# Hybrid attention and SSD block on one core: one C-times-B product per group, values of two heads in one product, state product ahead of the transposes, fourth tile's state products and last normalisation later

## The chip, the cores and the metric

The kernel runs on one core of one Trainium2 chip. The core has five engines with a queue each: TensorE (PE, matrix products), VectorE (DVE), ScalarE (ACT), GpSimd (POOL) and SyncE (SP, which issues the transfers). Each works through its own instructions in order; they wait for each other by semaphores. Time is device time of one execution in microseconds (us), lower is better. Products write into PSUM, eight banks of 128 partitions by 512 floats (2 KB); all else lies in SBUF.

## The reference

One layer over 512 positions of width 1024, in float32:

```python
u = rmsnorm(h, mix_pre_norm)
q, k, v, z, xbc, dt_raw, g_a, g_b = split(u @ w_in)
y_attn = banded_sink_attention(rope(q), rope(k), v, sinks) @ w_attn_out   # 16 heads, 4 groups, window 128
# SSD branch, 32 heads of 64 in 4 groups, state 128:
xs, B, C = split(silu(causal_dwconv(xbc)))
dt = softplus(dt_raw + bias); a_cs = cumsum(dt * a)          # within a chunk
y_diag = ((C @ B.T) * exp(a_cs[l] - a_cs[s]), lower triangle) @ (x * dt)
states = B.T @ (x * dt * decay);  prev = scan(prev * chunk_decay + states)
y_off  = (C @ prev) * exp(a_cs)
y = group_rmsnorm((y_diag + y_off + x * d_skip) * silu(z)) * ssd_norm
y_ssd = y @ w_ssd_out
h = h + rmsnorm((sigmoid(g_a) * y_attn + sigmoid(g_b) * y_ssd) @ w_out)
h = h + rmsnorm((silu(conv(gate)) * conv(value)) @ w_down)   # channel mixer, d_ff 2816
```

## The kernel before

**Tiling.** The 512 positions are four tiles (`NT` = 4) of 128. Each big product is made of three passes: weights are split on chip into a rounded high half `whi` (ScalarE, L482, function `hi`) and a rest `wlo` (VectorE, L863, function `lo`), and so are the activations. Weight blocks of 128x2048 come through two buffers `raw0`, `raw1`; block n can be split when it has landed and when TensorE has finished with block n-2 in that buffer. The semaphore `lo_done` counts finished low halves.

**Group loop.** Attention and SSD run in four groups (`NG` = 4; 4 query heads and 8 SSD heads each), Python loops that write each engine's instructions out in order. A group projects q, k, v (two weight blocks, a product group per tile), then B, C, x with their convolution, then turns B and x to rows of positions (`tok`). Then comes the tile loop, t = 0 to 3, in which TensorE does for each tile:

- `C times B` (L1552) into bank 6, masked by VectorE (`masked_cb`, L1090) into `cb_m`;
- the attention scores (L1565, four products) into banks 4 and 5;
- a quarter of the gate projection z (`z_tile`, 24 products of 512 columns), for t = 0 also the rest of `tok`;
- `turn_p`: the transposes of the probabilities (L1410) into bank 4, copied to `pT` by ScalarE (L692);
- for t > 0 the state products (L1393 with `c_dec` and `state`): the carried state times C scaled by growth;
- the decay products (L1393 with `decay_m` and `xdt`, `diagonal`), which end the tile's y (semaphore `y_mm`);
- for t < 3 the state product (L1589): B times `xdtd`, into bank 7, for the carried state;
- `weigh_values` (L1422): values times `pT`, eight products of 64 columns, into bank 4, copied to `oT` by ScalarE (L696).

The decay and values products have 64 columns of weights and write to partitions 0 to 63 and 64 to 127 in turn.

**The other engines.** After `y_mm` ScalarE makes the next tile's gains from the summed decays (L569, L575). VectorE takes the maximum of the scores (L1071 to L1074), multiplies the gains by `cb_m` (L1062), makes `xdt` = x times dt (L1086), divides the probabilities (L1078 to L1080), forms the gate (L1054), adds up y (L1113) and updates the state: times its decay (L1120), plus bank 7 (L1121). GpSimd makes `xdtd` (L439) and `c_dec`, C times growth for the next tile (L444), for which it waits until the tile's `y_mm`. The fourth tile's scores and state products come last in the group's loop; its decay products, transposes and values are laid between the next group's first projection tiles.

**After the groups.** `gate_a(i)`, i = 0 to 3: gate products (banks 0, 1) and attention-output products (banks 2, 3), 24 each, i = 0 outside and the others in a loop on every engine. The attention outputs `oT` are split into `rhi`, `rlo` first, then the SSD outputs `yT` (`split_y`, L1134), tiles 0 to 7 of them before the loop and 8 to 15 behind it. The last group's normalisation (`sum_squares`, `norm_sums`, roots by GpSimd, a trip of the roots through DRAM to spread them, `normalize` L977) stands in VectorE's queue behind `gate_a(0)`, ahead of the low halves of i = 1. Then come the SSD output products, the merge, w_out and the channel mixer, which are unchanged.

## Time and profile before

| | |
|---|---|
| median of 3 runs | 1061.54 us (1061.15 to 1063.48) |
| profiled execution, its own time | 1061.45 us |
| its span (first to last instruction) | 1059.7 us |
| mean granted TensorE clock | 0.996 |
| TensorE products busy | 1033.1 us (97%), 5423 records |
| VectorE busy | 640.1 us (60%) |
| ScalarE busy | 472.4 us (45%) |
| GpSimd busy | 86.9 us (8%) |
| mean of the low halves (L863) | 2.24 us |

The span is what the trace covers; the time has 1.75 us more around it. A product in plain float32 leaves two records in the trace, a product of the rounded halves one. Ends of products are modelled, so neighbouring rows overlap and a stretch is best measured from start to start.

### The profile page before, as it was taken

What the parts mean: (1) busy time and instruction counts of PE and PEld (TensorE: products, weight loads), DVE (VectorE), ACT (ScalarE), POOL (GpSimd) and SP (SyncE); (2) the same over time, 40 slices, a digit from 0 to 9 for tenths busy, and PEclk for the clock granted to TensorE, in tenths of its full rate; (3) what the DMA queues carried; (4) which work ended last, traced back from release to release, by engine and by line L of the source; (5) the groups of instructions that cost most, each with busy time, mean ns of one, the idle gap of its engine ahead of it and who ended that gap; (6) DMA issues with size and microseconds to landing.
All of it is one profiled execution on the core that took longest, in us unless ns stands there. A gap on an engine that the chain in (4) does not pass through costs nothing.

```text
span 1059.7 us, 14004 instructions
## 1 busy us (share of the span) xinstructions
PE 1033.1 (97%) x5423; PEld 863.8 (82%) x5423; DVE 640.1 (60%) x851; ACT 472.4 (45%) x835; POOL 86.9 (8%) x132
## 2 busy tenths in 40 slices
PE   8999999999999999989999999999999999999997
PEld 7887888798779877768888888798888888888886
DVE  4878787878787878642523223676766666651214
ACT  5657647655764576512312132554344343422112
POOL 6002101200120021000000003110000000000001
PEclk9999999999999999989999999999999999999999
DMA  6333351343334323232232344421243333332211
GB/s 193 120 126 109 111 148 50 118 133 109 97 103 143 106 100 120 50 111 87 87 112 79 119 158 152 127 71 50 79 114 83 97 101 82 116 119 80 98 62 79
DMA packets 117978, 111.26 MB, mean 105 GB/s; under 512 B 13279, under 2 KB 108075, under 8 KB 117931
## 3 DMA queue, kind: packets, MB, share of 16 engines
q1 hardware_dynamic: 117931, 110.61, 33.8%
q8 instruction: 32, 0.52, 0.2%
q14 instruction: 15, 0.12, 0.0%
HBM read 108.36 MB, written 2.24 MB: 104 GB/s over the span
## 4 chain that ended last, share of the span: by engine, by line
PE 88%; DVE 5%; ACT 3%; DMA 2%; issue 1%; POOL 1%; SPq 0%; DVEq 0%; POOLq 0%; ACTq 0%
PE ps L1292 20%; PE ps L1294 20%; PE ps L1293 20%; PE ps L1299 7%; PE ps L1301 6%; PE ps L1300 6%; PE ps L1393 2%; PE ps L1565 1%; DVE wlo L863 1%; DVE sm L1078 1%; PE ps L1589 1%; DVE state L1120 1%; PE ps L1422 1%; PE ps L1410 1%; ACT x_tok L557 1%
## 5 line engine op out<-in xcount | busy, mean ns | idle before, releaser
L863 DVE TENSOR_TENSOR wlo<-raw,whi 128x2048 fp32r<-128x2048 f32 (+2 forms) x83 | 185.9, 2242 | 198.3 <-ACT whi L482 198.3
L1292 PE MATMUL ps<-uhi,whi 128*128 128x512 f32 x768 | 301.4, 393 | 0.0
L1294 PE MATMUL ps<-uhi,wlo 128*128 128x512 f32 x768 | 299.2, 390 | 0.0
L1293 PE MATMUL ps<-ulo,whi 128*128 128x512 f32 x768 | 298.9, 389 | 0.0
L482 ACT ACTIVATE whi<-raw 128x2048 fp32r<-128x2048 f32 (+2 forms) x83 | 155.8, 1878 | 187.6 <-PE ps L1301 99.0
L1294 PEld LDWEIGHTS ps<-uhi,wlo 128*128 128x128 f32 x768 | 144.2, 188 | 30.4
L1293 PEld LDWEIGHTS ps<-ulo,whi 128*128 128x128 f32 x768 | 144.3, 188 | 29.1
L1292 PEld LDWEIGHTS ps<-uhi,whi 128*128 128x128 f32 x768 | 144.3, 188 | 29.2 <-issue 0.2
L1240 DVE SCALAR_TENSOR_TENSOR yT<-ps,fpar,yT 128x511 f32<-128x511 f32 x88 | 65.8, 749 | 37.5 <-ACT yT L820 35.9
L1292 PE MATMUL ps<-rhi,whi 128*128 128x512 f32 x192 | 75.8, 395 | 6.2 <-DVE wlo L863 6.2
L820 ACT ACTIVATE yT<-ps,fpar 128x512 f32<-128x512 f32 x44 | 34.2, 780 | 98.9 <-DVE fpar L1235 68.0
L1293 PE MATMUL ps<-rlo,whi 128*128 128x512 f32 x192 | 75.6, 394 | 0.0
L1294 PE MATMUL ps<-rhi,wlo 128*128 128x512 f32 x192 | 75.4, 393 | 0.0
L1299 PE MATMUL ps<-whi,rhi 128*128 128x512 f32 x176 | 68.5, 389 | 0.0
L1300 PE MATMUL ps<-whi,rlo 128*128 128x512 f32 x176 | 68.5, 389 | 0.0
L1301 PE MATMUL ps<-wlo,rhi 128*128 128x512 f32 x176 | 68.5, 389 | 0.0
L991 DVE SCALAR_TENSOR_TENSOR conv<-ps,par,conv 128x511 f32<-128x511 f32 (+2 forms) x72 | 53.9, 748 | 18.2 <-ACT conv L545 16.5
L1299 PE MATMUL ps<-whi,uhi 128*128 128x384 f32 (+2 forms) x176 | 64.2, 365 | 0.6 <-DVE wlo L863 0.6
L1301 PE MATMUL ps<-wlo,uhi 128*128 128x384 f32 (+2 forms) x176 | 62.7, 357 | 0.0
L1300 PE MATMUL ps<-whi,ulo 128*128 128x384 f32 (+2 forms) x176 | 62.6, 356 | 0.0
L545 ACT ACTIVATE conv<-ps,par 128x512 f32<-128x512 f32 x24 | 18.7, 778 | 68.7 <-PE ps L1294 68.7
L1292 PEld LDWEIGHTS ps<-rhi,whi 128*128 128x128 f32 x192 | 36.6, 190 | 14.2 <-DVE wlo L863 6.6
(226 smaller groups left out, 1370.5 us busy)
## 6 DMA issues: line engine op xcount, KB each, us to landing
raw<-in_w_in_dram SPq DMA_DIRECT2D x24, 1024.0 KB
raw<-in_w_up_dram SPq DMA_DIRECT2D x44, 512.0 KB
raw<-in_w_down_dram SPq DMA_DIRECT2D x11, 1024.0 KB
raw<-in_w_in_dram SPq DMA_DIRECT2D x16, 512.0 KB
sums_bc<-sum_rows_scratch SPq DMA_DIRECT2D x16, 512.0 KB, 4.2
raw<-in_w_ssd_out_dram SPq DMA_DIRECT2D x8, 1024.0 KB
grow_bc<-sum_rows_scratch SPq DMA_DIRECT2D x12, 512.0 KB, 5.7
raw<-in_w_attn_out_dram SPq DMA_DIRECT2D x4, 1024.0 KB
```

Source lines behind the costliest of these rows:

```text
L482: act.activation(whi[sl][:, 0:width] if into is None else into, raw[sl][:, 0:width], ACT.Copy).then_inc(s["hi_done"], 1)
L820: act.activation(work[:, v, :], bank(2 * q + v), ACT.Identity, scale=fpar[:, q, FTAPS - 1, v:v + 1], bias=fpar[:, q, FTAPS, v:v + 1]).then ...
L863: dve.tensor_tensor(wlo[sl][:, 0:width] if into is None else into, raw[sl][:, 0:width], h.bitcast(F32), ALU.subtract).then_inc(s["lo_done" ...
L991: ins = dve.scalar_tensor_tensor(out=conv[:, f, sh:], in0=ps[:, 4 + f % 4, 0:S - sh], scalar=cw[:, k, at:at + 1], in1=conv[:, f, sh:], op0 ...
L1240: ins = dve.scalar_tensor_tensor(out=work[:, v, sh:], in0=ps[:, 2 * q + v, 0:S - sh], scalar=fpar[:, q, k, v:v + 1], in1=work[:, v, sh:], ...
L1292: pe.matmul(bank(b)[:, span], hi_[:, k, c], ah[:, span], start=first and k == 0, stop=False)
L1293: pe.matmul(bank(b)[:, span], hi_[:, k, c], al[:, span], start=False, stop=False)
L1294: ins = pe.matmul(bank(b)[:, span], lo_[:, k, c], ah[:, span], start=False, stop=last and k == KD - 1)
L1299: pe.matmul(o, ah, wh, start=first, stop=False)
L1300: pe.matmul(o, al, wh, start=False, stop=False)
L1301: return pe.matmul(o, ah, wl, start=False, stop=last)
L1393: ins = pe.matmul(ps[r, 2 + t % 2, (h // 2) * P:(h // 2 + 1) * P], weights[:, h * HD:(h + 1) * HD], moving[:, h, :], start=first if t == 0 ...
```

## The change

Seven edits, all in the attention and SSD stage and in `gate_a`.

1. C times B for all four tiles is done in one batch of four products into bank 6, after `tok(1)`, and VectorE masks the four at once into `cb_m`, which now lies in the q columns of `qkv_sb`.
2. `weigh_values` does two heads in one product: four products of 2x64 columns instead of eight of 64. They go to bank 6, so the next scores wait for `pT_sb` only, no longer for `o_sb`.
3. The state product (L1589) moves from behind the decay products to right behind `z_tile`, ahead of `turn_p`.
4. The fourth tile's state products (`from_state`) move from behind its scores to right in front of its decay products, behind the next group's first projection tile. A new semaphore `off_mm` marks their end.
5. VectorE scales the state (`scaled`) as soon as `off_mm` is there, before the sum into yT. GpSimd's `c_dec` waits for `scaled` where it waited for `y_mm`, and at a group's first tile also for the low half of the block that VectorE splits there.
6. VectorE's order in a tile is maximum, masked gains, x times dt, division, gate in all tiles; at t = 0 the gate came before the division. ScalarE does the first gate's tanh ahead of its copies.
7. In the last group and `gate_a`: the products `features(1, ...)` stand between `turn_p` and `weigh_values`; five of the attention outputs are split earlier (`O_ORDER`); VectorE's order is gate_a(0), split_y 0 to 7, gate_a(1), normalize, gate_a(2), split_y 8 to 13, gate_a(3), split_y 14 and 15. `Y_TILE` gives the split SSD outputs 8 to 13 tiles of their own, so that they need not wait for the attention products to end. The loops of VectorE and ScalarE over i are written out.

TensorE's queue between the first and second tile of the second group, before (`whi`, `wlo` gate products end; names as above):

```order
L1294 MATMUL ps<-uhi,wlo 128x512
L1410 MATMUL ps<-ident,probs 128x128 x4
L1393 MATMUL ps<-decay_m,xdt 64x128 x8
L1589 MATMUL ps<-xdtd,b_tok 128x512
L1422 MATMUL ps<-pT,qkv_sb 64x64
L1422 MATMUL ps<-pT,va 64x64
...
L1552 MATMUL ps<-conv 128x128
L1565 MATMUL ps<-kB,qB 128x128 x4
```

and in the changed kernel:

```order
L1321 MATMUL ps<-uhi,wlo 128x512
L1616 MATMUL ps<-xdtd,b_tok 128x512
L1437 MATMUL ps<-ident,probs 128x128 x4
L1420 MATMUL ps<-decay_m,xdt 64x128 x8
L1453 MATMUL ps<-pT,qkv_sb 64x2x64 x2
L1453 MATMUL ps<-pT,va 64x2x64 x2
L1603 MATMUL ps<-kB,qB 128x128 x4
```

The state product has moved ahead of the transposes, the values are four instructions instead of eight, and C times B (L1552) is gone from between values and scores.

VectorE's queue in `gate_a`, with what each row waits for. Before, from the first block's gates to the first low half of the second block:

```order
L1153 SCALAR_TENSOR_TENSOR oT<-gt,ps 128x512 [waits at_mm,ga_tanh]
L1153 SCALAR_TENSOR_TENSOR oT<-gt,ps 128x512 [waits blk_done,ga_tanh]
L977 TENSOR_TENSOR yT<-yT,conv 128x512 [waits roots_in]
L977 TENSOR_TENSOR yT<-yT,conv 128x512 x3
L1134 SCALAR_TENSOR_TENSOR rlo<-yT,par,rhi 128x512 [waits split_hi] x4
...
L863 TENSOR_TENSOR wlo<-raw,whi 128x2048 [waits hi_done]
```

and now:

```order
L1170 SCALAR_TENSOR_TENSOR oT<-gt,ps 128x512 [waits at_mm,ga_tanh]
L1170 SCALAR_TENSOR_TENSOR oT<-gt,ps 128x512 [waits blk_done,ga_tanh]
L1156 SCALAR_TENSOR_TENSOR rlo<-yT,par,rhi 128x512 [waits split_hi] x8
L887 TENSOR_TENSOR wlo<-raw,whi 128x2048 [waits hi_done] x2
L1170 SCALAR_TENSOR_TENSOR oT<-gt,ps 128x512 [waits at_mm,ga_tanh]
L1170 SCALAR_TENSOR_TENSOR oT<-gt,ps 128x512 [waits blk_done,ga_tanh]
L1001 TENSOR_TENSOR yT<-yT,conv 128x512 [waits roots_in]
L1001 TENSOR_TENSOR yT<-yT,conv 128x512 x3
```

The normalisation (`roots_in`) has moved behind the low halves and gates of the second block.

The diff, cut to its core:

```diff
@@ semaphores, names
-        cb_m = sb("cb_m", [P, P], where=gctx)
+        cb_m = qkv_sb[:, :, 0:P]
+        O_ORDER = (1, 2, 3, 4, 5, 0, 6, 7)
+        Y_TILE = tuple(range(KD)) + tuple(range(2 * KD, KF)) + tuple(range(KD, 2 * KD + KI - KF))
@@ gpsimd
-                    pool.wait_ge(s["y_mm"], T + 1 if t else T)
+                    if t:
+                        pool.wait_ge(s["scaled"], G * (NT - 2) + t)
+                    else:
+                        pool.wait_ge(s["y_mm"], T)
+                        pool.wait_ge(s["lo_done"], G * PER_G + 7)
                     pool.tensor_tensor(c_dec[:, :, :], grow_bc[:, :, :], ...
@@ scalar
+            hi_gate(0)
+            square_y(NG - 1)
+            gates_a(0)
+            act.wait_ge(s["yn_ok"], KD)
+            for k in range(KD):
+                split_y(k)
             mean_y(NG - 1)
+            for i in range(1, NG):
+                hi_attention(i)
+                gates_a(i)
+                hi_gate(i)
+                if i == 2:
+                    act.wait_ge(s["yn_ok"], KI)
+                    for k in range(KD, KF - KD):
+                        split_y(k)
@@ vector, after silu(5)
+                dve.wait_ge(s["cb_mm"], G + 1)
+                dve.tensor_tensor(cb_m, bank(6).rearrange("p (t l) -> p t l", t=NT), tri..., ALU.mult).then_inc(s["cbm_ok"], 1)
@@ vector, tile loop
+                    if 0 < t < NT - 1:
+                        dve.wait_ge(s["off_mm"], G * (NT - 1) + t)
+                        dve.tensor_tensor(h8(state[:, :]), h8(state[:, :]), heads(dec[:, 2, t, group_heads(G)], SH, HD),
+                                          ALU.mult).then_inc(s["scaled"], 1)
+                        dve.wait_ge(s["scaled"], G * (NT - 2) + t)
+                        dve.wait_ge(s["st_mm"], G * (NT - 1) + (t + 1))
+                        dve.tensor_tensor(state[:, :], state[:, :], bank(7), ALU.add).then_inc(s["st_ok"], 1)
                     dve.wait_ge(s["y_mm"], T + 1)
@@ tensor
+                for half in (1, 0):
+                    cols = slice(64 * half, 64 * half + 64)
+                    v = qkv_sb[:, t, QW + KW:QW + 2 * KW] if half else va[:, t, :]
+                    for a in range(2):
+                        o = ps[64 * a:64 * a + 64, 6, 0:2 * P].rearrange("p (f c) -> p f c", f=2)[:, :, cols]
+                        ins = pe.matmul(o, v, pT[:, 2 * a:2 * a + 2, cols], start=True, stop=True)
+            def from_state(G, t):
+                T = G * NT + t
+                pe.wait_ge(s["st_ok"], G * (NT - 1) + t)
+                pe.wait_ge(s["grown"], G * (NT - 1) + t)
+                if T > 1:
+                    pe.wait_ge(s["y_done"], T - 1)
+                if t == 1:
+                    pe.wait_ge(s["tok_sb"], G * 5 + 3)
+                products(G, t, state, c_dec, True, False).then_inc(s["off_mm"], 1)
@@ tensor, next group's first tile
                         if h == 0 and t == 0:
+                            from_state(G - 1, NT - 1)
                             diagonal(G - 1, NT - 1)
@@ tensor, after tok(1)
+                for t in range(NT):
+                    c = slice(t * P, (t + 1) * P)
+                    ins = pe.matmul(ps[:, 6, c], conv[:, 0, c], conv[:, 1, c], start=True, stop=True)
+                ins.then_inc(s["cb_mm"], 1)
@@ tensor, tile loop
-                        pe.wait_ge(s["o_sb"], T)
+                        pe.wait_ge(s["pT_sb"], T)
...
                         pe.matmul(bank(7), b_tok[:, c], xdtd[:, :], start=True, stop=True).then_inc(s["st_mm"], 1)
+                        turn_p(G, t)
+                        if t:
+                            from_state(G, t)
+                        diagonal(G, t)
                         weigh_values(G, t)
```

## Rows read from the trace of the kernel before

**Rows 1.** Waits of TensorE: waiter, released by: us in total, times, longest

```profile
PE ps L1292 <- DVE wlo L863: 6.2, 1, 6.2
PE ps L1393 <- DVE state L1121: 3.1, 4, 1.2
PE ps L1410 <- DVE probs L1080: 2.6, 4, 0.7
...
PE ps L1422 <- ACT pT L692: 0.7, 1, 0.7
```

**Rows 2.** Timeline, TensorE, second group, first tile: start, us, instruction, [idle before]

```profile
183.69 0.39 PE L1293 MATMUL ps<-ulo,whi 128*128 128x512 f32 x1
183.91 0.39 PE L1294 MATMUL ps<-uhi,wlo 128*128 128x512 f32 x1
184.96 0.66 PE L1410 MATMUL ps<-ident,probs 128*128 128x128 f32 x4 [0.66 <-DVE probs L1080]
185.54 1.09 PE L1393 MATMUL ps<-decay_m,xdt 128*64 128x128 f32 x16
186.57 1.12 PE L1589 MATMUL ps<-xdtd,b_tok 128*128 128x512 f32 x2
187.62 0.34 PE L1422 MATMUL ps<-pT,qkv_sb 128*64 128x64 f32 x4
...
188.29 0.49 PE L1552 MATMUL ps<-conv 128*128 128x128 f32 x2
188.88 1.13 PE L1565 MATMUL ps<-kB,qB 128*128 128x128 f32 x8
189.76 0.48 PE L1292 MATMUL ps<-uhi,whi 128*128 128x512 f32 x1
```

**Rows 3.** Timeline, VectorE, second group

```profile
181.55 2.41 DVE L1078 TENSOR_TENSOR sm<-sm 128x4 f32<-128x4 f32 x1 [0.60 <-ACT sm L663]
...
205.16 1.44 DVE L1080 TENSOR_TENSOR probs<-probs,sm 128x512 f32<-128x512 f32 x1
...
210.30 2.14 DVE L1120 TENSOR_TENSOR state<-state,dec 128x512 f32<-128x512 f32 x1
...
214.48 1.29 DVE L1062 TENSOR_TENSOR decay_m<-decay_m,cb_m 128x512 f32<-128x512 f32 x2
215.69 0.68 DVE L1086 TENSOR_TENSOR xdt<-x_tok,dt_s 128x512 f32<-128x512 f32 x1
```

**Rows 4.** Timeline, GpSimd, second group

```profile
181.53 2.41 POOL L444 TENSOR_TENSOR c_dec<-grow_bc,conv 128x1024 f32<-128x1024 f32 x1
...
205.00 1.04 POOL L439 TENSOR_TENSOR xdtd<-xdt,dec 128x512 f32<-128x512 f32 x1 [4.65 <-DVE xdt L1086]
```

**Rows 5.** Timeline, TensorE, second group, fourth tile

```profile
211.45 1.13 PE L1565 MATMUL ps<-kB,qB 128*128 128x128 f32 x8
213.22 1.09 PE L1393 MATMUL ps<-c_dec,state 128*64 128x128 f32 x16 [0.64 <-DVE state L1121]
```

**Rows 6.** Timeline, ScalarE, gains of the fourth tile

```profile
209.34 1.28 ACT L569 ACTIVATE decay_m<-sums_bc,sum_s 128x128 f32<-128x128 f32 x4 [1.39 <-PE ps L1393]
210.97 0.38 ACT L696 ACTIVATE oT<-ps 128x256 f32<-128x256 f32 x1 [0.34 <-PE ps L1422]
...
212.41 1.14 ACT L575 ACTIVATE decay_m<-decay_m 128x512 f32<-128x512 f32 x2
```

**Rows 7.** Timeline, TensorE, the long wait of the last group

```profile
455.38 0.80 PE L1292 MATMUL ps<-rhi,whi 128*128 128x512 f32 x1 [6.18 <-DVE wlo L863]
455.97 0.63 PE L1293 MATMUL ps<-rlo,whi 128*128 128x512 f32 x1
```

**Rows 8.** Chain that ended last, 434 to 456: start, us, what

```profile
441.23 5.19 DMA conv<-roots_scratch
...
447.43 3.04 DVE yT L977 x3
```

**Rows 9.** Windows: busy us of each engine, granted clock (PEclk), DMA share, GB/s

```profile
core 0: us, PE busy (x) PEld busy (x) DVE busy (x) ACT busy (x) POOL busy (x), PEclk, DMA share, GB/s
...
455.00:461.00 6.00, 5.62 (x15) 4.44 (x16) 2.52 (x2) 0.00 (x0) 0.00 (x0) 0.57 0.76 249
```

More of the change, by code:

```diff
@@ L688, in group @@
                         hi_next(7, 4 * QKV if G < NG - 1 else BLK)
+                        if G == NG - 1:
+                            for k in O_ORDER[0:5]:
+                                split_o(k)
                     else:
@@ L705, in _, with split_y, gates_a @@
             act.wait_ge(s["o_sb"], NG * NT)
-            for k in range(KD):
-                act.activation(rhi[:, KD + k, :], oT[:, k, :], ACT.Copy).then_inc(s["split_hi"], 1)
+            for k in O_ORDER[5:]:
+                split_o(k)
             SN = 0
-            act.wait_ge(s["yn_ok"], KD)
-            for k in range(KD):
-                act.activation(rhi[:, k, :], yT[:, k, :], ACT.Copy, scale=par[:, 1, SN + k:SN + k + 1]).then_inc(s["split_hi"], 1)
-            square_y(NG - 1)
-            def gate_a(i, first=False):
+            def split_y(k):
+                act.activation(rhi[:, Y_TILE[k], :], yT[:, k, :], ACT.Copy, scale=par[:, 1, SN + k:SN + k + 1]).then_inc(s["split_hi"], 1)
+            def gates_a(i):
                 n = i * 2 + N_C1
-                if not first:
-                    hi(1, 64 * (i + (N_C1 // 2 + 1)), n)
                 for m in range(2):
@@ L1114, in group @@
                                       ALU.add).then_inc(s["y_done"], 1)
-                    if t < NT - 1:
-                        dve.wait_ge(s["st_mm"], G * (NT - 1) + (t + 1))
-                        if t == 0:
-                            dve.tensor_copy(state[:, :], bank(7)).then_inc(s["st_ok"], 1)
-                        else:
-                            link(dve.tensor_tensor(h8(state[:, :]), h8(state[:, :]), heads(dec[:, 2, t, group_heads(G)], SH, HD), ALU.mult))
-                            dve.tensor_tensor(state[:, :], state[:, :], bank(7), ALU.add).then_inc(s["st_ok"], 1)
+                    if t == 0:
+                        dve.wait_ge(s["st_mm"], G * (NT - 1) + 1)
+                        dve.tensor_copy(state[:, :], bank(7)).then_inc(s["st_ok"], 1)
                 if G < NG - 1:
@@ L1152, in gate_a @@
                         dve.wait_ge(s["blk_done"], n + 2)
-                    dve.scalar_tensor_tensor(out=oT[:, bass.ds(i * 2 + m, 1), :], in0=gt[:, m:m + 1, :], scalar=1.0,
+                    dve.scalar_tensor_tensor(out=oT[:, i * 2 + m:i * 2 + m + 1, :], in0=gt[:, m:m + 1, :], scalar=1.0,
                                              in1=ps[:, 2 + m:3 + m, :], op0=ALU.add, op1=ALU.mult).then_inc(s["at_ok"], 1)
-            gate_a(0, True)
-            normalize(NG - 1)
-            for k in range(KD // 2, KD):
-                split_y(k, KD + k + 1)
-            with dve.Fori(1, NG) as i:
-                gate_a(i)
-            for k in range(KD, KI):
-                split_y(k, KD + k + 1)
+            for at in range(5):
+                split_o(at)
+            gate_y(NG - 1)
+            for at in range(5, KD):
+                split_o(at)
+            lo(0, N_C1 + 3)
+            sum_squares(NG - 1)
+            gate_a(0)
+            for k in range(KD):
+                split_y(k)
+            gate_a(1)
+            normalize(NG - 1)
+            gate_a(2)
+            for k in range(KD, KF - KD):
+                split_y(k)
+            gate_a(3)
+            for k in range(KF - KD, KI):
+                split_y(k)
             before = links["n"]
@@ L1284, in tiles, with features @@
                 return w.rearrange("p (k n) -> p k n", k=k)
-            def features(b, sl, m, acts, first=True, last=True, span=slice(0, S), split=None):
+            def features(b, sl, m, acts, first=True, last=True, span=slice(0, S), split=None, ks=tuple(range(KD))):
                 hi_, lo_ = (tiles(w, KD) for w in split or (whi[sl][:, :], wlo[sl][:, :]))
-                for k in range(KD):
+                for k in ks:
                     ah, al = acts(k)
                     c = slice(m * P, (m + 1) * P)
-                    pe.matmul(bank(b)[:, span], hi_[:, k, c], ah[:, span], start=first and k == 0, stop=False)
+                    pe.matmul(bank(b)[:, span], hi_[:, k, c], ah[:, span], start=first and k == ks[0], stop=False)
                     pe.matmul(bank(b)[:, span], hi_[:, k, c], al[:, span], start=False, stop=False)
-                    ins = pe.matmul(bank(b)[:, span], lo_[:, k, c], ah[:, span], start=False, stop=last and k == KD - 1)
+                    ins = pe.matmul(bank(b)[:, span], lo_[:, k, c], ah[:, span], start=False, stop=last and k == ks[-1])
                 return ins
@@ L1522, in tok @@
                     else:
-                        pe.wait_ge(s["cbm_ok"], G * NT + 1)
+                        pe.wait_ge(s["cbm_ok"], G + 1)
                     for t in range(NT):
```

122 lines of the change are left out of this document (48 added, 74 removed).

## The prediction

> **What bounds the kernel now.** I read the page's engine table, then the view of waits for TensorE, then TensorE's rows in order of time around each wait, and last the other engines in the same stretches. The reader is to see that TensorE is busy nearly all of the 1059.7 us, so that time can only go where it has no product to run, where it runs a product badly packed, or where its clock is low. The profiled execution took 1061.45 us and the median of the runs is 1061.54 us, so sums made on the trace carry over as they are.
>
> The waits are few [rows 1]: one of 6.2 us for the low half of a weight block, four for the state (3.1 us in all), four for the probabilities (2.6 us) and one of 0.7 us for the turned probabilities. Everything between them is products back to back. Ends of products are modelled, so I measure by starts: neighbouring 512-column products start 0.23 us apart [rows 2].
>
> **Part 1: state product first, at a group's first tile.** The transposes of the probabilities start 1.05 us after the last gate product where 0.23 is ordinary: 0.82 us lost, in each of four groups [rows 2]. VectorE finishes the probabilities late because a 128x4 addition took 2.41 us [rows 3], exactly while GpSimd ran its 2.41 us scaling of C [rows 4]. The change puts the 512-column state product in this place. It needs only xdtd, which GpSimd had finished when it started on C, 3.4 us before the transposes began. And GpSimd's scaling of C now waits for the low half of a weight block, so the addition is free of it. I take all of 4 x 0.82 = 3.3 us. Late next would again be the probabilities: the addition may now wait for GpSimd's 1.04 us for xdtd instead of 2.41, its queue is shorter by the gate (0.7), and the transposes come 0.9 us later behind the state product, so some 2 us are left to them.
>
> The Trainium skill, in SBUF — State Buffer, section on port contention rules, says that GpSimd and a VectorE instruction with two SBUF inputs take the shared port pair as a lock for the whole instruction, and the later one blocks fully. The trace agrees (2.41 beside 2.41). By that rule the scaling of C is harmless in its new place too, since the gate, the sum into yT and the copy of the state each read PSUM for one input; a rule that blocked all of VectorE would cost up to 2.4 us of VectorE time a group there.
>
> **Part 2: the fourth tile's state products later.** After the scores of the fourth tile (211.45) the state products start at 213.22, 1.77 us later, where four score products cost 0.88 [rows 2, 5]: 0.88 lost. Rows 1 give 3.1 us for the four by modelled ends, 0.64 for this one; with 0.24 added to each that is 4.1 us. The cause is the state's scaling on VectorE, 2.14 us instead of some 0.7, again beside GpSimd [rows 3]. Afterwards the state is scaled before GpSimd may start, and the products stand behind one tile of projection (twelve products of 384 columns, 12 x 0.17 = 2.1 us and 0.2 of changes; in the last group a block of 24, 5.5 us). All 4.1 us go.
>
> But the products with the decay follow at once, and used to have this projection tile between them and the state products as well as before them. They need the gains. ScalarE's chain from the first gain (209.34) to the last exponential (213.55) is 4.21 us, with 0.34 of waiting for the values' copy that goes [rows 6], so about 3.85; then half of the masking (0.65 of 1.29) and x times dt (0.6 more) [rows 3]: 5.1 us. ScalarE starts 0.2 us after TensorE ends the third tile's decay products, so they can run 5.3 us after that end. TensorE gets there after values 0.56, scores 0.95, projection tile 2.3 and state products 0.93: 4.7 us. **New wait** 0.6 us in three groups (0 to 1.0 each): minus 1.8 us. In the last group the 5.5 us block covers it. Queued behind it on TensorE is everything; nothing else on its queue could run.
>
> Also, state and decay products now stand side by side, which saves two changes of array layout per group. One change costs about 0.1 us (below); with the slow first product after each, 0.25 a group, 1.0 us (0 to 1.4).
>
> **Part 3: C times B once per group.** Now one such product stands alone in each tile: 188.29 to 188.88, 0.59 us, the last 0.2 to 0.3 of it waiting for the values' copy out of bank 4, which the scores overwrite [rows 2]. The values go to bank 6 now, so this wait goes with it. Twelve of these leave (tiles two to four): 7.1 us. They return in the group's batch at the price of a score product, 0.88 / 4 = 0.22: 12 x 0.22 = 2.6. The scores then come directly behind 64-column products and pay the exposed weight load that C times B paid: I take 0.07 each, 0.8 in all (0 to 1.2). Net 7.1 - 2.6 - 0.8 = 3.7 us. VectorE masks all four at once, which lies under the 5.6 us of gate products.
>
> **Part 4: layout changes around the state product.** It stands between two groups of 64-column products and takes 1.05 us (186.57 to 187.62), where four products of 128 columns, the same columns, take 0.88 [rows 2]. The 0.17 is what two changes of layout cost it; the decay products before it pay about 0.1 more at their end. Moved behind the gate products and ahead of the transposes it has full-width neighbours. 12 x (0.17 + 0.1) = 3.3 us; from 0 (if 512 columns cost that anywhere) to 3.6.
>
> The Trainium skill, TensorEngine Tiling (Array Packing), section Key Properties, says a change of tiling mode drains the engine while a change of tile does not. By it the 3.3 us stand; without it only the part that is not a drain would, nearly 0. The row (0.17 us over) leans to the rule.
>
> **Part 5: values of two heads together.** Sixteen records of 64 columns take 0.67 us (187.62 to 188.29). Sixteen of 128 columns in the decay products take 1.03 (185.54 to 186.57), pairs side by side [rows 2]; eight of them take half of 0.93 and 0.1 for the layout: 0.56. 16 tiles x 0.11 = 1.8 us (0 to 2).
>
> **Part 6: the last group.** The 0.7 us wait for the turned probabilities [rows 1] gets a block of products laid between: 0.7 us.
>
> The large one: TensorE waits 6.18 us by the modelled end, 0.39 - 0.23 more by starts, 6.34 us, until 455.38 [rows 7]. VectorE's low half is queued behind the normalisation, which waits for a broadcast of the roots, 5.19 us from 441.23, and then spends 3.04 on three of its four products [rows 8] and four splittings more. After the wait TensorE starts products 0.43 apart, and its granted clock is 0.57 over the 6 us from 455 [rows 7, 9]: some are at 1.2 GHz, the engine having been idle just before. To 460.2 that is 12 products, 2.35 us more than at 0.23. Afterwards VectorE does the second block's low half before the normalisation, and the roots are then long there. I follow the queues for the next thing to be late: the low half for the attention products of the second block is due 11 us after its gate products start (436 to 447 on the old clock); ahead of it stand eight splittings of the size of x times dt [rows 3] (8 x 0.7 = 5.6 us) and its own 2.3 (a bound, that of the table's 2.24 us mean), so it is ready about 443 to 444. Slack 3 us. The normalisation's outputs are first used by ScalarE two blocks later. 6.34 + 2.35 = **8.7 us**.
>
> **Sum.** 3.3 + 4.1 - 1.8 + 1.0 + 3.7 + 3.3 + 1.8 + 0.7 + 8.7 = 24.8 us. 1061.45 - 24.8 = **1036.7 us**. With every unknown at its better end 1032; with all at the worse end 1045.
>
> **Rivals.**
> A. GpSimd loses the lock. For the state product GpSimd must multiply xdt by the decay (1.04 us) while VectorE divides the probabilities. Before, GpSimd came first: the multiplication by the inverse sum took 1.44 us beside it [rows 3, 4]. If VectorE is first, GpSimd ends up to 1 us later. From the end of the decay products, xdtd is due after 0.56 + 0.95 + 5.6 = 7.1 us and is ready at 5.3 + 0.1 + 1.04 = 6.4; one more and TensorE waits 0.3 to 0.4 at 12 tiles: 4 us, 1041. For it: the slack is only 0.7. Against: xdt ends before the last exponential that the division needs. By the rule of the Trainium skill cited in part 1 it would be a whole instruction that GpSimd waits for.
> B. The end wait is only moved: the low half for the second block slips by more than its 3 us of slack (ScalarE has eight splittings and four squares in front). A wait of 3 us and again the low clock, 2.35: 1042. Against: no transfer is ahead of it.
> C. Layout changes and values give nothing (3.3 + 1.8 + 1.0 lost): 1043. For it: none of these is a measured alternative; against, 0.17 and 0.11 are in the rows.
> D. Slower. The path from the decay products through gains, mask, xdt and GpSimd to the state product becomes the bound. It used to have state product, values and C times B beside it, 2.3 us; now only the values lie ahead of the scores. It has 0.7 us of slack; the change is a loss once each of twelve tiles waits over 24.8 / 12 = 2.1 us, so the path would have to be 2.8 us longer than the 6.4 its rows give, from GpSimd and VectorE blocking each other two or three times a tile. At 3 us a tile: 1073.
> E. The change does not do what it says, since a wait left in place holds the old order (the copy of the values to bank 6 against the transposes there, say): near 1058.
>
> **How the numbers follow.** Forecast 0.74, A 0.08, B 0.06, C 0.07, D 0.03, E 0.02. The range reaches A, B and C: 1031.5 to 1044. Time within 0.2% (2.1 us) cannot be told from no change. Faster by more than that: all but D and part of E, 0.95; same 0.02; slower 0.03.
>
> **What would show it.** Right: no idle ahead of the first tile's transposes, nor after the fourth tile's scores; 0.3 to 1 us ahead of the fourth tile's decay products in three groups; state product at 0.9 us, values at 0.56, C times B eight records in 0.9; clock at 1.00 from 437 to 467; no release by the normalisation. Wrong: TensorE waiting for GpSimd's xdtd at each tile (A or D), for a low half near 440 (B), or the state product still at 1.05 (C).

## The result and the profile after

| | before | changed |
|---|---|---|
| median | 1062.32 us, 4 runs (1061.15 to 1063.48) | 1036.14 us, 4 runs (1035.75 to 1037.94) |
| profiled execution, its own time | 1061.45 us | 1036.33 us |
| its span | 1059.7 us | 1034.5 us |
| mean granted TensorE clock | 0.996 | 0.998 |

The ratio of the times is 0.9757, with a 95% interval of 0.974 to 0.9774. 1036.7 us had been forecast, 24.8 us less than the profiled execution before; the profiled execution took 25.1 us less, and the medians differ by 26.2 us. The forecast stood on a median of 1061.54 us over three runs; with the fourth it is the 1062.32 us of the table.

The page first: the engine table and TensorE's clock in 40 slices.

```profile
PE 1019.5 (99%) x5295; PEld 860.9 (83%) x5295; DVE 622.3 (60%) x839; ACT 470.3 (45%) x835; POOL 86.4 (8%) x132
...
PEclk9999999999999999999999999999999999999999
```

TensorE's waits in the changed kernel (us in total, times, longest), without three of the kind of the last ones:

```profile
PE ps L1420 <- DVE xdt L1112: 2.4, 3, 0.8
PE ps L1343 <- POOL ones L373: 2.0, 1, 2.0
PE ps L1319 <- DVE ulo L907: 1.8, 2, 1.0
...
PE ps L1372 <- ACT uhi L499: 0.5, 1, 0.5
```

All four entries of [rows 1] are gone. One is new, the first: the products with the decay wait for x times dt, three times. The others stand in the start and at the change of stage, as before. The view lists idle time by modelled ends, and a wait of some 0.15 us does not show in it.

TensorE in the second group, from the first tile's gate products to the next ones (start, us, instruction). It answers to [rows 2]:

```profile
181.21 0.39 PE L1321 MATMUL ps<-uhi,wlo 128*128 128x512 f32 x1
181.44 1.02 PE L1616 MATMUL ps<-xdtd,b_tok 128*128 128x512 f32 x2
182.29 0.60 PE L1437 MATMUL ps<-ident,probs 128*128 128x128 f32 x4
182.82 1.09 PE L1420 MATMUL ps<-decay_m,xdt 128*64 128x128 f32 x16
183.75 0.39 PE L1453 MATMUL ps<-pT,qkv_sb 128*64 128x128 f32 x4
183.97 0.39 PE L1453 MATMUL ps<-pT,va 128*64 128x128 f32 x4
184.28 1.16 PE L1603 MATMUL ps<-kB,qB 128*128 128x128 f32 x8
185.20 0.48 PE L1319 MATMUL ps<-uhi,whi 128*128 128x512 f32 x1
```

No row has an idle mark. By starts: state product 0.85 us (1.05 before), decay products 0.93 (1.03), values 0.53 (0.67), scores 0.92. From the first of these to the next gate product it is 3.76 us; before, it was 4.80 for the same work with C times B, and 0.82 of waiting ahead of it. C times B is eight records at another place, from 167.39 to 168.21.

The fourth tile of the second group, TensorE, where [rows 5] stood:

```profile
204.63 1.16 PE L1603 MATMUL ps<-kB,qB 128*128 128x128 f32 x8
205.54 0.42 PE L1326 MATMUL ps<-whi,uhi 128*128 128x384 f32 x1
...
207.83 1.09 PE L1420 MATMUL ps<-c_dec,state 128*64 128x128 f32 x16
209.71 1.09 PE L1420 MATMUL ps<-decay_m,xdt 128*64 128x128 f32 x16 [0.79 <-DVE xdt L1112]
```

The projection follows the scores after 0.91 us, without a wait. The decay products start 1.88 us after the state products, which themselves need 0.93: the new wait is 0.95 us. The other two groups that have it show the same 1.88 us between the two starts.

VectorE in the same group: first the first tile, then the scaling of the state in the second, then the fourth tile (answers to [rows 3]):

```profile
178.36 0.16 DVE L1104 TENSOR_TENSOR sm<-sm 128x4 f32<-128x4 f32 x1
...
178.77 1.32 DVE L1106 TENSOR_TENSOR probs<-probs,sm 128x512 f32<-128x512 f32 x1
...
193.26 0.69 DVE L1131 TENSOR_TENSOR state<-state,dec 128x512 f32<-128x512 f32 x1 [1.01 <-PE ps L1420]
...
207.67 1.29 DVE L1088 TENSOR_TENSOR decay_m<-decay_m,qkv_sb 128x512 f32<-128x512 f32 x2 [0.55 <-ACT decay_m L584]
208.88 0.68 DVE L1112 TENSOR_TENSOR xdt<-x_tok,dt_s 128x512 f32<-128x512 f32 x1
```

The 128x4 addition is back to 0.16 us and the scaling of the state to 0.69. What stayed is the multiplication by the inverse sum beside GpSimd's xdtd (178.50 to 179.54), 1.32 us where 0.69 is its length alone (210.07). The masking waits for ScalarE, and x times dt ends at 209.56 with TensorE waiting.

The last group, in windows (busy us of each engine, then TensorE's granted clock, DMA share, GB/s), as [rows 9]:

```profile
421.00:427.00 6.00, 6.00 (x32) 5.08 (x31) 5.86 (x9) 2.76 (x4) 1.84 (x2) 1.00 0.02 2
427.00:445.00 18.00, 18.00 (x81) 14.89 (x80) 6.36 (x6) 4.28 (x4) 0.00 (x0) 1.00 0.58 190
```

TensorE is busy in all of both and its clock is full. The wait of [rows 7] and the slow stretch behind it are gone. The low half that TensorE waited for there is this one now:

```profile
427.05 2.28 DVE L887 TENSOR_TENSOR wlo<-raw,whi 128x2048 fp32r<-128x2048 f32 x1
```

It ends at 429.33, and TensorE starts the products that need it at 432.70. From the start of the second block's gate products to the start of the third block's it is 21.90 us; before, it was 30.64, 8.74 more.

### The profile page after: what moved, and what is told of

It reads as the page before. It is cut to its first block, busy times and chain, and to the rows that moved or that the text cites. A ratio compares the mean times of both kernels' runs of the same rounds, so it can differ in the third digit from the quotient of the medians.

```text
span 1034.5 us, 13679 instructions
## 1 busy us (share of the span) xinstructions
PE 1019.5 (99%) x5295; PEld 860.9 (83%) x5295; DVE 622.3 (60%) x839; ACT 470.3 (45%) x835; POOL 86.4 (8%) x132
## 4 chain that ended last, share of the span: by engine, by line
PE 92%; ACT 2%; DVE 2%; DMA 1%; POOL 1%; issue 1%; SPq 0%; DVEq 0%; POOLq 0%; ACTq 0%
PE ps L1319 22%; PE ps L1321 21%; PE ps L1320 21%; PE ps L1326 6%; PE ps L1328 6%; PE ps L1327 6%; PE ps L1420 2%; PE ps L1603 1%; PE ps L1616 1%; PE ps L1567 1%; ACT decay_m L578 1%; PE ps L1437 1%; PE ps L1453 1%; DMA raw<-in_w_in_dram 1%; DMA raw<-in_w_up_dram 1%
## 5 line engine op out<-in xcount | busy, mean ns | idle before, releaser
L1015 DVE SCALAR_TENSOR_TENSOR conv<-ps,par,conv 128x511 f32<-128x511 f32 (+2 forms) x72 | 53.9, 748 | 18.2 <-ACT conv L554 16.5
L578 ACT ACTIVATE decay_m<-sums_bc,sum_s 128x128 f32<-128x128 f32 x128 | 40.3, 390 | 13.2 <-PE ps L1420 13.2
```

What stands on the lines that cost most here:

```text
L578: ins = act.activation(decay_m[:, h, :], sums_bc[:, h, :], ACT.Relu, scale=-1.0, bias=sum_s[:, t, at:at + 1])
L1015: ins = dve.scalar_tensor_tensor(out=conv[:, f, sh:], in0=ps[:, 4 + f % 4, 0:S - sh], scalar=cw[:, k, at:at + 1], in1=conv[:, f, sh:], op0 ...
```

## The experiments

Each was timed against the kernel before on the same chip. Line numbers shift by a few from kernel to kernel.

**pool_late** is the kernel before with one line added, which keeps GpSimd's scaling of C at a group's first tile behind a low half of VectorE.

```diff
                     pool.wait_ge(s["y_mm"], T + 1 if t else T)
+                    if t == 0:
+                        pool.wait_ge(s["lo_done"], G * PER_G + 7)
```

> The kernel before, with one wait added: GpSimd's scaling of C at a group's first tile also waits for the low half of the sixth weight block. If the 2.41 us addition was held up by GpSimd (my theory), the probabilities are ready about 182.5 in the second group, the transposes follow the gate products without the 0.82 us, and four groups give 3.3 us: about 1059.0 against 1062.3. If VectorE was late for another reason (ScalarE's exponentials), the wait stays and the time is that of before, within 0.5 us.

Measured: 1058.49 us (1058.12 to 1059.43), ratio 0.9962 (0.995 to 0.9975), that is 2.7 to 5.3 us less; span 1056.1. TensorE at the first tile:

```profile
183.26 0.39 PE L1296 MATMUL ps<-uhi,wlo 128*128 128x512 f32 x1
183.49 0.60 PE L1412 MATMUL ps<-ident,probs 128*128 128x128 f32 x4
```

The transposes start 0.23 us after the last gate product in all four groups, where it was 1.05, and take 0.53 us instead of 0.59: 3.5 us by the trace, 3.6 by the spans. The three other entries of [rows 1] stand as they were. The cause (the addition beside GpSimd, [rows 3, 4]) and the size are shown.

One wait outlives the edit that neither [rows 1] nor the forecast has, since it is too short for the view. The third tile's transposes, in the kernel before, second group:

```profile
206.27 0.39 PE L1294 MATMUL ps<-uhi,wlo 128*128 128x512 f32 x1
206.65 0.66 PE L1410 MATMUL ps<-ident,probs 128*128 128x128 f32 x4
```

They start 0.38 us after the last gate product instead of 0.23 and take 0.59 instead of 0.53, right as the 1.44 us multiplication of [rows 3] ends (206.60). That is 0.21 us in each group, in pool_late too; in the changed kernel the state product stands in this place and it is gone.

**no_lo_wait** is the changed kernel without GpSimd's added wait for the low half.

```diff
                         pool.wait_ge(s["y_mm"], T)
-                        pool.wait_ge(s["lo_done"], G * PER_G + 7)
```

> The changed kernel without that added wait. Lock theory: GpSimd scales C right behind xdtd, 2.4 us, and the multiplication of the probabilities (waiting since 178.8) ends near 182.6, 0.4 us too late for the transposes; everything VectorE does behind it is 2.4 us later too, which may reach the next tile's state product. 1.5 to 5 us slower than the changed kernel: 1037.6 to 1041. Rival, that the state product ahead of the transposes covers all by itself: no difference, 1036.

Measured: 1036.48 us (1036.16 to 1038.06), ratio 0.9758 (0.9738 to 0.9778), span 1034.6. A miss: I expected a loss and there is none. VectorE, then GpSimd, at the first tile:

```profile
178.16 0.16 DVE L1103 TENSOR_TENSOR sm<-sm 128x4 f32<-128x4 f32 x1
...
178.58 1.31 DVE L1105 TENSOR_TENSOR probs<-probs,sm 128x512 f32<-128x512 f32 x1
...
180.41 3.88 DVE L886 TENSOR_TENSOR wlo<-raw,whi 128x2048 fp32r<-128x2048 f32 x1
```

```profile
178.29 1.05 POOL L441 TENSOR_TENSOR xdtd<-xdt,dec 128x512 f32<-128x512 f32 x1 [43.91 <-DVE xdt L1111]
179.30 2.85 POOL L449 TENSOR_TENSOR c_dec<-grow_bc,conv 128x1024 f32<-128x1024 f32 x1
```

The addition takes 0.16 us and ends as GpSimd begins on xdtd, and the probabilities are done at 179.89, as early as with the wait (180.09, in an execution that stands 0.21 us later). The low half pays instead, 3.88 us for 2.28, and nobody waits for it. The new order of the engines alone does all of part 1; the added wait is a second cure for the same loss, needed only in the old order. The rows say how. Before, ScalarE did the gate's tanh at 179.42, just ahead of the exponentials, and their sums came at 181.52, when VectorE had waited 0.60 us for them and GpSimd was starting on C (181.53). Now the tanh stands at 173.94, the sums are there when x times dt is done, and the addition (178.16 in no_lo_wait) comes 1.1 us ahead of the scaling of C (179.30). The probabilities are done over a microsecond before the gate products end, so the state product is not needed for it. The tanh and the place of the gate were not tried one by one.

**st_back** puts the state product back behind the decay products.

```diff
                         z_tile(t + 1)
+                        turn_p(G, t)
+                        if t:
+                            from_state(G, t)
+                        diagonal(G, t)
                         pe.wait_ge(s["xdtd_ok"], G * (NT - 1) + t + 1)
...
-                        turn_p(G, t)
-                        if t:
-                            from_state(G, t)
-                        diagonal(G, t)
                         weigh_values(G, t)
```

> The changed kernel with the state product back behind the decay products. The probabilities are ready at 180.1, before the gate products end at 181.4, so no wait comes back. Layout theory: the state product takes 1.05 instead of 0.86 us and the decay products 0.1 more, 12 tiles: 3.5 us, 1039.6. Rival (the move only hid the wait for the probabilities, which is gone by the other edit): 1036, state product at 0.86 as well.

Measured: 1038.74 us (1038.5 to 1039.05), ratio 0.9774 (0.9757 to 0.9792). The interval overlaps that of the changed kernel, so the time alone does not tell them apart. The trace does (TensorE, second group, second tile):

```profile
193.11 1.04 PE L1420 MATMUL ps<-decay_m,xdt 128*64 128x128 f32 x16
194.09 1.12 PE L1620 MATMUL ps<-xdtd,b_tok 128*128 128x512 f32 x2
195.14 0.44 PE L1453 MATMUL ps<-pT,qkv_sb 128*64 128x128 f32 x4
```

The state product takes 1.05 us again (0.85), the decay products 0.98 (0.87 in this tile), the values 0.59 (0.54). That is 0.35 us a tile, 4.2 us in twelve tiles. 1.9 us come back, since the new wait shrinks from 0.95 to 0.32 us three times: the gains of the fourth tile start when the third tile's decay products end, and the third state product now lies beside them, not ahead of them. Net 2.3 us; the medians differ by 2.6.

**vals_eight** does the values again in eight products, in bank 6.

```diff
-                for half in (1, 0):
-                    ...
-                    for a in range(2):
-                        ... pe.matmul(o, v, pT[:, 2 * a:2 * a + 2, cols], ...)
+                for h in range(QH):
+                    for half in (1, 0):
+                        ... pe.matmul(o, v, pT[:, (h % 2) * 2 + h // 2, 64 * half:64 * half + 64], ...)
```

> The changed kernel with the values as eight products of 64 columns into bank 6. They take 0.66 instead of 0.54 us in 16 tiles: 2.0 us, 1038.1. Rival (same columns, so the same time): 1036.

Measured: 1038.69 us (1037.61 to 1039.81), ratio 0.9771 (0.9751 to 0.9791). The values run from 185.53 to 186.14 at the first tile, 0.61 us against 0.54: 16 x 0.075 = 1.2 us from the pairing, where 2.0 had been expected. The span of the profiled execution, 1038.0 us, is 3.5 us longer than the changed kernel's. Of the rest, 1.5 us lie before the first group's scores and 0.7 behind the groups, where the two kernels are alike, so I do not put them down to the edit.

**cb_each** does C times B once per tile again, ahead of the scores, into bank 5 beside the sums; the values stay in bank 6.

```diff
...
-                for t in range(NT):
-                    c = slice(t * P, (t + 1) * P)
-                    ins = pe.matmul(ps[:, 6, c], conv[:, 0, c], conv[:, 1, c], start=True, stop=True)
-                ins.then_inc(s["cb_mm"], 1)
...
+                    pe.matmul(ps[:, 5, 2 * P:3 * P], conv[:, 0, c], conv[:, 1, c], start=True, stop=True)
                     for h in range(QH):
```

> The changed kernel with C times B back in every tile, as one product directly ahead of the scores, in spare columns of bank 5, and masked by VectorE after the scores; the values stay in bank 6. My theory now: the batch by itself saves next to nothing, since the product costs 0.22 us in either place and the first of a run behind 64-column products pays the exposed load whichever it is. Same time within 0.7 us: 1035.5 to 1036.8; the wait ahead of the fourth tile's decay products may grow. Rival (the batch is what saved, 12 times 0.59 less 2.6): about 4.4 us slower, 1040.5.

Measured: 1036.07 us (1035.64 to 1036.23), ratio 0.976 (0.9744 to 0.9777), span 1033.8. TensorE, second group:

```profile
192.89 0.39 PE L1451 MATMUL ps<-pT,qkv_sb 128*64 128x128 f32 x4
193.11 0.39 PE L1451 MATMUL ps<-pT,va 128*64 128x128 f32 x4
193.43 0.49 PE L1595 MATMUL ps<-conv 128*128 128x128 f32 x2
193.75 1.06 PE L1598 MATMUL ps<-kB,qB 128*128 128x128 f32 x8
```

C times B takes 0.32 us here, not the 0.59 of [rows 2], and the scores behind it 0.81 where they take 0.92 behind the values: 0.32 - 0.11 = 0.21, the price in the batch (0.81 / 4 = 0.20). So the batch saves nothing, and the first full-width product behind the values pays 0.11 us more, whichever it is. The weight loads in the changed kernel's trace fit this: that of the first score product starts at 184.28 together with its product, those of the next start 0.11 us ahead of theirs. C times B and scores together took 0.59 + 0.88 = 1.47 us a tile before and take 1.13 here: 0.34 us in twelve tiles, 4.1 us.

**o_bank4** keeps the batch and puts the values back into bank 4; the next scores wait for their copy again.

```diff
-                                   bank(6, 2 * P).rearrange(...), ACT.Copy, scale=0.5).then_inc(s["o_sb"], 1)
+                                   bank(4, 2 * P).rearrange(...), ACT.Copy, scale=0.5).then_inc(s["o_sb"], 1)
...
-                        o = ps[64 * a:64 * a + 64, 6, 0:2 * P]...
+                        o = ps[64 * a:64 * a + 64, 4, 0:2 * P]...
...
                     if t:
-                        pe.wait_ge(s["pT_sb"], T)
+                        pe.wait_ge(s["o_sb"], T)
```

> The changed kernel with the values back in bank 4, so that the next scores wait for ScalarE's copy of them; the batch stays. My theory: bank 6 carries the gain. ScalarE does half of the gains (1.28 us) ahead of that copy, and state product and C times B no longer stand in between, so the scores start near 185.7 instead of 184.3 in the second group's second tile: 1.4 us in 12 tiles, 17 us, about 1053. If the copy came directly behind the values it would be 0.5 us each, 1042. Rival (the batch carries it): 1036 to 1038.

Measured: 1051.88 us (1050.82 to 1052.86), ratio 0.9911 (0.9895 to 0.9928), span 1049.2. TensorE at the second tile's end, then ScalarE there:

```profile
198.62 0.39 PE L1453 MATMUL ps<-pT,va 128*64 128x128 f32 x4
200.34 1.13 PE L1603 MATMUL ps<-kB,qB 128*128 128x128 f32 x8 [1.34 <-issue]
```

```profile
198.70 1.28 ACT L578 ACTIVATE decay_m<-sums_bc,sum_s 128x128 f32<-128x128 f32 x4 [1.39 <-PE ps L1420]
199.88 0.36 ACT L708 ACTIVATE oT<-ps 128x256 f32<-128x256 f32 x1
```

There are twelve such waits, 16.0 us by modelled ends. The profile names no releaser, but the scores start at 200.34, 0.10 us after ScalarE ends the copy, and the edit put back the wait for it. The copy stands in ScalarE's queue behind 1.28 us of gains, which before were covered by the state product. With the state product moved, the values end before the gains do. Twelve times 1.41 us by starts are 17 us, of which 1.9 come back at the new wait, which shrinks to 0.33 us: 15, and 15.7 by the medians.

**state4_back** puts the fourth tile's state products right behind its scores.

```diff
+                    if t == NT - 1:
+                        from_state(G, t)
                     if t < NT - 1:
...
                         if h == 0 and t == 0:
-                            from_state(G - 1, NT - 1)
                             diagonal(G - 1, NT - 1)
...
                 if first:
-                    from_state(NG - 1, NT - 1)
                     diagonal(NG - 1, NT - 1)
```

> The changed kernel with the fourth tile's state products back right behind its scores, the decay products where they are. They must wait for GpSimd's scaling of C, which ends at 206.7 while the scores end at 205.5: 1.1 us in four groups, and 0.3 us for two more layout changes; but the wait of 0.95 us ahead of the decay products goes in three groups. Net 2.4 us slower, 1038.5. Rival (the move is worth its full 4.1 + 1.0 us and the new wait is of another cause): 1041.

Measured: 1039.22 us (1039.02 to 1041.56), ratio 0.9789 (0.9772 to 0.9805). TensorE, then GpSimd, second group:

```profile
206.83 1.16 PE L1602 MATMUL ps<-kB,qB 128*128 128x128 f32 x8
208.96 1.09 PE L1420 MATMUL ps<-c_dec,state 128*64 128x128 f32 x16 [0.97 <-issue]
...
212.27 1.09 PE L1420 MATMUL ps<-decay_m,xdt 128*64 128x128 f32 x16
```

```profile
206.50 2.36 POOL L450 TENSOR_TENSOR c_dec<-grow_bc,conv 128x1024 f32<-128x1024 f32 x1 [3.70 <-DVE state L1131]
```

The profile names no releaser; the state products start 0.10 us after GpSimd ends its scaling of C (208.86), as expected, and in the last group too.

1.2 us are lost behind the scores in each of the first three groups and 1.9 in the last, 5.5 in all, and the wait ahead of the decay products (2.9) is gone: 2.6 net. From the first scores to the end of the groups the trace is 3.2 us longer, which leaves 0.6 us for the separated state and decay products; the medians differ by 3.1.

**norm_back** puts the normalisation ahead of the low halves of the second block.

```diff
             gate_a(0)
+            normalize(NG - 1)
             for k in range(KD):
...
             gate_a(1)
-            normalize(NG - 1)
```

> The changed kernel with VectorE's last normalisation back ahead of the low halves of the second block of gate_a, eight splittings between. The roots land near 430.5, normalisation 3.4, splittings 5.5, low half 2.3: ready at 441.7, where TensorE wants it at 432.6. 9 us of waiting and 2.3 us of products at 1.2 GHz behind it: 11.4 us slower, 1047.5. Rival (TensorE keeps its clock): 9 us. Rival (the wait was for ScalarE or a transfer): 1036.

Measured: 1048.44 us (1047.31 to 1049.95), ratio 0.9873 (0.9856 to 0.9889). TensorE, then VectorE, then the window behind the wait:

```profile
434.73 0.39 PE L1321 MATMUL ps<-uhi,wlo 128*128 128x512 f32 x1
443.91 0.80 PE L1319 MATMUL ps<-rhi,whi 128*128 128x512 f32 x1 [8.79 <-DVE wlo L887]
```

```profile
432.34 4.01 DVE L1001 TENSOR_TENSOR yT<-yT,conv 128x512 f32<-128x512 f32 x4 [8.26 <-DMA conv<-roots_scratch]
436.25 5.40 DVE L1156 SCALAR_TENSOR_TENSOR rlo<-yT,par,rhi 128x512 fp32r<-128x512 f32 x8
```

```profile
444.00:450.00 6.00, 6.00 (x18) 4.76 (x19) 2.06 (x1) 0.00 (x0) 0.00 (x0) 0.64 0.87 285
```

8.95 us of wait and a clock of 0.64 behind it, as in [rows 7, 9] only longer, since all eight splittings now stand behind the normalisation, four more of 0.68 us than before. From the start of the second block's gate products to the start of the third block's it is 33.07 us, 11.2 more than the 21.90 of the changed kernel: 8.95 of waiting and 2.2 of slow products. The medians differ by 12.3 us.

The last three look for the new wait. **xdt_first** does x times dt ahead of the masking in the fourth tile; **diag_later** moves the fourth tile's state and decay products, transposes and values one projection tile later; **both_waits** is both.

```diff
-                    masked_gains()
-                    times_dt()
+                    if t == NT - 1:
+                        times_dt()
+                        masked_gains()
+                    else:
+                        masked_gains()
+                        times_dt()
```

```diff
-                        if h == 0 and t == 0:
+                        if h == 0 and t == 1:
                             from_state(G - 1, NT - 1)
                             diagonal(G - 1, NT - 1)
-                        elif h == 0 and t == 1:
-                            turn_p(G - 1, NT - 1)
                         elif h == 0 and t == 2:
+                            turn_p(G - 1, NT - 1)
+                        elif h == 0 and t == 3:
                             weigh_values(G - 1, NT - 1)
```

> The changed kernel; at the fourth tile VectorE makes x times dt before it masks the gains, while it waits for the exponentials anyway. The decay products then wait for the mask only, which ended at 208.96 where x times dt ended at 209.57: 0.6 us in three groups, 1.8 us faster, 1034.3. Rival (VectorE's queue is full there, so that the mask ends later by what x times dt takes): no difference.

> The changed kernel; the fourth tile's state and decay products stand behind the second projection tile of the next group instead of the first, transposes and values one tile later too. The wait of 0.95 us in three groups is covered by 2.1 us of products: 2.9 us faster, 1033.2. Rival: the fourth projection tile, which overwrites the y bank, now waits for the sum into yT behind a low half in VectorE's queue (ready 213.4 where it would be wanted at 214.5, 1.1 us of slack): 0 to 3 us back.

> Both of the edits above. If the later place covers the wait whole, x times dt first adds nothing: 1033.2, as with the later place alone. If a rest of the wait is left there, this one is faster by it.

Measured: xdt_first 1034.22 us (1033.73 to 1036.15), ratio 0.9745 (0.9731 to 0.9758); diag_later 1033.52 (1032.85 to 1035.75), 0.9743 (0.973 to 0.9756); both_waits 1033.4 (1032.74 to 1034.11), 0.9739 (0.9725 to 0.9752). TensorE at the fourth tile's state and decay products, in xdt_first and then in diag_later:

```profile
208.78 1.09 PE L1424 MATMUL ps<-c_dec,state 128*64 128x128 f32 x16
209.97 1.09 PE L1424 MATMUL ps<-decay_m,xdt 128*64 128x128 f32 x16
```

```profile
208.47 1.09 PE L1420 MATMUL ps<-c_dec,state 128*64 128x128 f32 x16
209.40 1.04 PE L1420 MATMUL ps<-decay_m,xdt 128*64 128x128 f32 x16
```

The wait goes from 0.95 to 0.27 us and to nothing. From the start of the first scores to the first attention-output product behind the groups the traces take 331.11 us in the changed kernel, 329.11 in xdt_first and 328.20 in diag_later and in both_waits. So 2.0 and 2.9 us of the new wait can be had back, and x times dt first adds nothing to the later place. In diag_later the view of waits has none for the sum into yT, so its rival did not come. The medians lie 1.9, 2.6 and 2.7 us below the changed kernel's. The intervals of the ratios overlap, so the times alone tell none of the three from the changed kernel or from each other.

## Why the prediction was right

Most of the mechanisms held, with two corrections: the new wait was longer than worked out, and the gain of part 3 comes from the bank of the values and not from the batch. That the sum came within 0.6 us was partly luck. Two items fell short of the forecast by 1.5 us together, and five others, one of them not in the sum at all, went beyond it by 1.8.

First the stretches. The first tile's transposes of the first and fourth group stand 295.91 us apart before (86.32 and 382.23) and 285.14 after (87.25 and 372.39), 3.59 us less per group; the terms of parts 1 to 5 give 3.70 with the new wait. The first attention-output product behind the groups starts at 426.32 before and at 409.81 after, 16.5 us earlier; parts 1 to 5 and the small item of part 6 give 16.1. Those attention-output products then take 0.2 us more than before. From the second block's gate products to the third block's it is 8.74 us less, where 8.7 was forecast, and all that follows differs by 0.1 us.

- **Part 1**, 3.3 us: 3.5, and pool_late shows the cause alone. The price of the added wait, up to 2.4 us of VectorE time a group, did not come up: beside GpSimd's scaling of C in its new place (183.06, 2.37 us) the gate (182.81) and the sum into yT (183.96) took 0.68 and 0.69 us, as elsewhere. That the added wait is superfluous beside the new order, I had not seen. Nor had I seen the third tile's late probabilities, 0.21 us in each group: 0.8 us that the sum lacks.
- **Part 2**, 4.1 us: all gone. That GpSimd held up the state's scaling rests on rows (2.14 us beside it before, 0.69 now); no run brings the old wait back. The **new wait**, minus 1.8 us, is the mis-sized term: 3 x 0.95 = 2.9. Counted from the start of the values (204.09), TensorE got there after 4.67 us, where 4.74 had been worked out. But x times dt ended after 5.47 us, not 5.3, and the products started 0.15 us after that end, which I had not counted. The three differences are 0.07, 0.17 and 0.15 us, and 0.56 + 0.39 = 0.95. It lies inside the 0 to 1.0 stated. State and decay products side by side were put at 1.0 us; state4_back gives 0.6.
- **Part 3**, 3.7 us: 4.1, but the heading was wrong. cb_each shows that the batch saves nothing. The gain is the bank of the values: of the 0.59 us that C times B took, the part that could go was the wait for the values' copy, which I had read in the rows (0.2 to 0.3 us) but booked with the batch. And o_bank4 shows what I had missed: in the new order, without the other bank, the kernel would be 15.7 us slower. The step failed where it took that wait for an item of 0.2 to 0.3 us whatever else moves: the copy is queued behind the gains, and the moved state product lays that bare.
- **Part 4**, 3.3 us: the state product takes 0.85 us (0.88 forecast) and the decay products 0.1 less, 0.30 us in twelve tiles, 3.6. St_back gives 0.35 a tile; the further 0.05 is the first value product behind a full-width one. The Trainium skill, TensorEngine Tiling (Array Packing), section Key Properties, says that a change of tiling mode drains the engine. The rows agree as far as they go: 1.05 us for the state product between products of another layout, 0.85 between two of its own. They show the price of the change and not the drain itself.
- **Part 5**, 1.8 us: values 0.54 (0.56 forecast), 0.07 less in the fourth tiles: 1.8. Pairing is worth 1.2 of it by vals_eight; the rest is the layout change that part 4 moved away.
- **Part 6**: the transposes and values of the last group stood 1.34 us apart and do so no more, 0.8 us against the 0.7 forecast. The large item, 8.7 us, is 8.74: 6.35 of waiting and 2.39 of slow products. norm_back brings wait and low clock back. The low half of the second block came in time, with 3.4 us to spare where 3 had been worked out.
- **The range.** The unknowns as stated add up to 3.5 us on the better side, which is 1033.2 us and not 1032.
- **Rivals.** A: GpSimd came first (178.50, the multiplication 178.77), and no state product waited. B and D: no such wait in the view. C: the state product takes 0.85 us and the values 0.54, and both go back up in st_back and vals_eight. E: the waits of [rows 1] are gone.

The items as measured are 3.5 + 0.8 + 4.1 - 2.9 + 0.6 + 4.1 + 3.6 + 1.8 + 0.8 + 8.7 = 25.1 us, the 25.1 us between the two profiled executions. The division among them is read from the starts of products and was made after the result. The experiments bear out part 1, the bank of part 3, the move of part 4, the pairing of part 5, the large item of part 6 and the new wait; the 4.1 us of part 2 and the 0.8 us of the third tile have no run of their own.

## What to carry to other kernels

When a bank is shared, look at what stands ahead of its copy in the copying engine's queue: a move elsewhere can uncover it, and a spare bank is then worth far more than the wait that the old trace shows. Where a step has two edits that each cure the same wait, try them one by one, in both orders of the rest; here the added wait is needed in the old order only. Where work is moved off the stretch beside another engine's chain, count that chain from its first instruction to the start of the waiting product, the last 0.15 us too.

## What the runs showed of the hardware

Two GpSimd instructions stood back to back in no_lo_wait and a VectorE multiplication had been waiting since 178.58. It got in between them: it was done at 179.89, and GpSimd's second, begun at 179.30, took 2.85 us instead of the 2.37 of the changed kernel. In the kernel before, an addition of 128x4 that came after the start of the same GpSimd instruction waited for all of its 2.41 us [rows 3, 4]. So in these two cases it went by who had asked first: the multiplication was there 0.7 us before GpSimd's second instruction, the addition 0.02 us after it. A low half started 1.1 us into the GpSimd instruction took 3.88 us instead of 2.28, and ended 2.14 us after it.

A change of layout costs at both ends. The state product between two groups of 64-column products took 1.05 us against 0.85 between full-width ones, the decay products ahead of it 0.1 us more at their end, and the first interval of the value products behind it was 0.27 against 0.22 us: 0.35 us in all for one product laid between two groups.
